# Products of constants in TensorE's waits at six norms of a two-block transformer

## What is computed

```python
for layer in range(2):                       # first block
    h = rmsnorm(x, g_mix[layer])             # norm "mix0", "mix1"
    x = x + three_attention_branches(h @ w_in[layer]) @ w_out[layer]
    h2 = rmsnorm(x, g_mlp[layer])            # norm "mlp0", "mlp1"
    x = x + square(relu(h2 @ w_up[layer])) @ w_down[layer]
x = rmsnorm(x, g_final)                      # norm "final"
x = layer_norm(ALPHA * x + gated_deltanet(x), ln_g[0, 0], ln_b[0, 0])      # "ln00"
x = layer_norm(ALPHA * x + swiglu(x), ln_g[0, 1], ln_b[0, 1])              # "ln01"
x = layer_norm(ALPHA * x + window_attention(x), ln_g[1, 0], ln_b[1, 0])    # "ln10"
x = layer_norm(ALPHA * x + moe_swiglu(x), ln_g[1, 1], ln_b[1, 1])          # "ln11"
```

## Time and profile before

| | |
|---|---|
| median of 3 runs | 2503.48 us (2501.76 to 2505.6) |
| time of the profiled execution | 2501.3 us |
| its span | 2499.6 us |
| mean granted TensorE clock | 0.985 |
| TensorE busy | 2406.9 us of the span |
| VectorE, ScalarE, GpSimd busy | 1750.8, 1420.4, 137.5 us |

### The profile page before, as it was taken

One profiled execution on the slowest core, in us unless ns is written; L12 is line 12 of the kernel. 1 busy time (PEld: TensorE's weight loads), 2 busy tenths in 40 slices (PEclk: granted clock), 3 DMA queues, 4 the chain that ended last, 5 costly groups with the idle time before them and its releaser, 6 DMA issues. The chain is left out here.

```text
span 2499.6 us, 34680 instructions
## 1 busy us (share of the span) xinstructions
PE 2406.9 (96%) x13819; PEld 2051.7 (82%) x13819; DVE 1750.8 (70%) x2029; ACT 1420.4 (57%) x1629; POOL 137.5 (6%) x177
## 2 busy tenths in 40 slices
PE   7999899999998999998999889999999999999998
PEld 6797699888777998777998778888888888888886
DVE  4456655544676555576545578898889889988988
ACT  4544544453455444433444457777777777777776
POOL 0102200000121000050000000000000000000000
PEclk9999999999999999899999899999999999999999
DMA  8343445533344555405566339999999999999997
GB/s 294 106 148 123 168 177 197 182 135 113 131 148 179 185 202 140 100 1 186 171 196 197 104 118 318 366 365 366 367 366 366 363 363 364 364 357 357 366 365 252
DMA packets 392784, 585.54 MB, mean 234 GB/s; under 512 B 21232, under 2 KB 286896, under 8 KB 392496
## 3 DMA queue, kind: packets, MB, share of 16 engines
q1 hardware_dynamic: 392624, 583.33, 68.8%
HBM read 579.09 MB, written 4.19 MB: 233 GB/s over the span
## 5 line engine op out<-in xcount | busy, mean ns | idle before, releaser
L3588 DVE TENSOR_TENSOR moe_low<-ring,moe_high 128x2048 fp32r<-128x2048 f32 x288 | 658.5, 2289 | 90.3 <-ACT moe_high L3544 86.2
L3544 ACT CAST moe_high<-ring 128x2048 fp32r<-128x2048 f32 x288 | 548.3, 1907 | 140.7 <-PE bank L3472 69.7
L3472 PE MATMUL bank<-moe_high,moe_xh 128*128 128x512 f32 x896 | 239.7, 389 | 1.0 <-PEq L3186 1.0
L3472 PE MATMUL bank<-moe_low,moe_xh 128*128 128x512 f32 x896 | 239.9, 390 | 0.0
L3472 PE MATMUL bank<-moe_high,moe_xl 128*128 128x512 f32 x896 | 239.5, 389 | 0.0
L3472 PEld LDWEIGHTS bank<-moe_high,moe_xh 128*128 128x128 f32 x896 | 168.0, 188 | 36.0 <-issue 1.1
L3472 PEld LDWEIGHTS bank<-moe_high,moe_xl 128*128 128x128 f32 x896 | 168.2, 188 | 35.0
L3472 PEld LDWEIGHTS bank<-moe_low,moe_xh 128*128 128x128 f32 x896 | 168.2, 188 | 34.9
L2132 DVE TENSOR_TENSOR chain_low<-ring,chain_high 128x2048 fp32r<-128x2048 f32 x48 | 110.0, 2291 | 117.8 <-ACT chain_high L2105 117.8
L2105 ACT CAST chain_high<-ring 128x2048 fp32r<-128x2048 f32 x44 | 84.1, 1912 | 142.1 <-PE bank L2076 108.2
L3478 PE MATMUL bank<-moe_high,moe_hh 128*128 128x512 f32 x444 | 127.4, 408 | 0.6 <-DVE moe_hl L3623 0.6
(11 more groups left out here) (545 smaller groups left out, 4918.7 us busy)
## 6 DMA issues: line engine op xcount, KB each, us to landing
ring<-in_moe_w_gate SPq DMA_DIRECT2D x199, 512.0 KB, 6.3
ring<-in_moe_w_up SPq DMA_DIRECT2D x199, 512.0 KB, 8.3
ring<-in_moe_w_down SPq DMA_DIRECT2D x95, 1024.0 KB, 8.9
ring<-in_w_in SPq DMA_DIRECT2D x21, 2048.0 KB, 8.0
ring<-in_w_down SPq DMA_DIRECT2D x14, 2048.0 KB, 7.8
ring<-in_w_up SPq DMA_DIRECT2D x10, 2048.0 KB, 8.1
xT<-in_moe_w_down SPq DMA_DIRECT2D x17, 1024.0 KB, 8.6
xT<-in_moe_w_gate SPq DMA_DIRECT2D x31, 512.0 KB, 6.6
```

What stands on the lines that cost most here:

```text
L3472: mm = pe.matmul(core.banks[i % 2][:], (xl if other_low else xh)[:, place(m), 4 * part + c, :], wt[:, c, :], start=(part == 0 and j == 0 a ...
L3544: act.copy(unit(high, u), ring.raw(u)).then_inc(s["weight_high"], 1)
L3588: dve.tensor_tensor(unit(low, u), ring.raw(u), unit(high, u), ALU.subtract)\
```

## The change

`turn_rows` looks up a triple of counts for its norm in a new table: how many idle products stand ahead of the first turn, between the turns, and behind the second. Each place gets a bank of its own: ahead, the columns that the first transpose writes; between, the columns that the second turn's first transpose writes; behind, columns of the first of the other four banks. ln10 keeps its counts. mix0 (the start) has none.

```diff
+IDLE = {"mlp0": (0, 18, 3), "mix1": (0, 21, 12), "mlp1": (0, 18, 3), "final": (0, 21, 8), "ln00": (0, 28, 0),
+        "ln01": (50, 7, 10), "ln10": (0, 13, 13)}
...
-    def turn(self, pe, src, ready=None, idle=(0, 0, 0), idle_bank=None):
+    def turn(self, pe, src, ready=None, idle=(0, 0, 0), idle_banks=(None, None, None)):
...
             if ready is not None and k == 0:
-                idle_products(self.core, pe, idle_bank, idle[t])
+                idle_products(self.core, pe, idle_banks[t], idle[t])
                 pe.wait_ge(ready[t], 1)
...
-        idle_products(self.core, pe, idle_bank, idle[NT])
+        idle_products(self.core, pe, idle_banks[NT], idle[NT])
...
     def turn_rows(self, pe):
-        idle, bank = ((0, 13, 13), self.core.banks[0][:, 0:P]) if self.row == "ln10" else ((0, 0, 0), None)
-        self.turn(pe, self.dst, (self.s["normed0"], self.s["normed1"]), idle, bank)
+        turned, other = self.banks[0], self.core.banks[4 if self.banks[0] is self.core.banks[0] else 0]
+        self.turn(pe, self.dst, (self.s["normed0"], self.s["normed1"]), IDLE.get(self.row, (0, 0, 0)),
+                  (turned[:, 0:P], turned[:, P:2 * P], other[:, 0:P]))
```

## The result

The changed kernel takes 2513.68 us (median of 8 runs, 2511.18 to 2515.81), beside 2503.43 us for the kernel before (8 runs, 2497.71 to 2506.09). The ratio is 1.0048, 95% interval 1.0036 to 1.0059: slower by 9 to 15 us. 2512.9 us was forecast, in a range of 2507 to 2518. The number was right; one step of its sum was not. In the pair of profiled executions a chance difference of 5.2 us hid that, and the timed runs show only part of what the step left out, as told at the end.

The account below looks back on a forecast made before the run. TensorE was taken as the bound. Site terms 1.84 (mlp1) + 0.81 (mlp0) + 2.52 (ln00) + 0.79 (mix1) + 0.97 (final) + 2.50 (ln01) = 9.4 us, set on the 2503.48 us median, gave 2512.9 us, range 2507 to 2518.

Parts of the forecast that it names:

- TensorE is the bound and a late turn makes the end late: Whole kernel: TensorE, busy 96% of the span, bounds the end; lateness at an earlier norm reaches it unless something absorbs it.
- rival 3: Expert stage waits for its weights and makes good a late start: same time, about 2503.5 us; 4%.
- 0.224 us for a product, two records: Price of one idle product at full clock, from ln10's 13 products: 26 records in 3.07 us.
- Rival 1: At the norms, products fit the waits and the clock comes back: 9.3 us gained, about 2494 us; 4%.
- The formula that the prediction set beside the rows: Warm product as N/2.4 + 2.5 ns: 0.056 us for 128 columns, against 0.224 us from ln10's rows.
- The delays between the turns: Products exceeding the waits make second turns late: 1.84 us at mlp1, 1.85 at mlp0, 2.93 at ln00.
- The clock comes back: At norms with half-clock stretches, filled waits restore full clock; credits such as 1.04 us at mlp0, 0.41 at ln00.
- rival 2: At the norms the clock falls all the same; delays stay, credits go: 2520 us; 9%.
- one of the prediction's own signs of being wrong: The prediction is wrong if the clock is below 1.00 at mix1 and ln01.
- ScalarE's copies are in time: At mix1, copies don't delay the first product, 3.6 us after the turn's start; at final it came after 2.10.
- Rival 4: Only half the loss arrives, as half-clock stretches elsewhere vanish or copies pace the passes: 2506 to 2508 us; 5%.
- the bounds: Above: 2520.3 us without clock credit, worst 22.7 us added; below: pacing copies hide perhaps 1 us, half-clock shifts 3 to 5.

Follow-up runs that it names:

- The doubled site: The changed kernel with 36 products instead of 18 between the turns of mlp1; a single execution, 2519.77 us.
- the counts that fit: Against the kernel before: idle products sized at 0.224 us each to fit the waits, none behind except ln10's; 2491.96 us, ratio 0.9973; again 2494.21 us, 0.9969.
- the narrow ones: The changed kernel with products of 64 columns instead of 128, all counts as they are; 2517.62 us, ratio 1.0063 to the kernel before.

## Why the prediction was right, and where it was not

**TensorE is the bound and a late turn makes the end late:** right. The doubled site added 4.01 us at its place and none of it came back; rival 3 (a later stage takes it up) is out. From the expert stage's first product to the end of the span it is 992.9 to 993.0 us in all fourteen profiles.

**0.224 us for a product, two records:** right, 0.223. Rival 1 (the products fit) is out as a description of the change, but with counts for this price it is what happens: 0.3% faster, with 4 to 5 us at the sites of the 9 that it was given. The formula that the prediction set beside the rows (the Trainium skill, "TensorE: Matmul & The Clock Gate", section "Back-to-back issue gap") is given there for an isolated product, and the section says itself that it counts too little at small widths. The prediction was right to go by the rows.

**The delays between the turns:** right. mlp1 +1.62 for 1.84; ln00 +2.25 for 2.52. What is missing I had not taken off: the 25th product comes 4.69 us after a turn that follows other work (with or without products behind it) and 4.93 us after one that follows a wait, both at full clock.

**The clock comes back:** right in the first two executions of the change, at all six sites; rival 2 is out there. In the third, mix1 is at 0.91, one of the prediction's own signs of being wrong, and 1.3 us longer. So it is right in the main, and not each time.

**"ScalarE's copies are in time":** this step failed, for mix1, and with it the sums of final and ln01, which went by it. I took the copies to follow the transposes, since the timeline gives the release of TensorE by `x_high` and nothing about what releases `x_high`. The section on the kernel says the same, that each pair of transposes releases a copy. At mlp0, mlp1 and ln00 that is all; at mix1, final and ln01 the copies stand behind the barrier as well, and it is the later. With the products ahead of it, the 25th product comes 8.56 us (mix1), 7.46 (final) and 7.89 (ln01) behind the second turn. I had 6.3, 5.4 and 5.9: 3.59, 2.69 and 3.14 to the first product, and 2.73 for the next 24. The missing term is 2.2 + 2.0 + 2.0 = 6.3 us, before rounding: 1.1 to 1.4 at each because the copies start late, and 0.9 to 1.0 because the first pass then runs at their pace. In the timelines, taking the products away or past the barrier moved it as the barrier theory says. Rival 4 and the bounds had copies that pace the passes hide part of the delay; at these three norms they added to it. The kernel before already had the evidence, in ScalarE's timeline at mix1, which I had not asked for:

```profile
498.49 2.05 ACT L408 CAST x_high<-bank 128x512 fp32r<-128x512 f32 x4 [3.61 <-PEq L740]
```

The copies' wait is ended by TensorE's sequencer at the end of the block, 2.57 us after a turn that itself lasts 1.97. At mlp1, in the middle of a block, no such meeting stands between turn and copies, and there the products behind did cost nothing.

**Why the time was right all the same.** In the profiled pair it was luck. Forecast +9.4, the sites say 14.9 between the two first profiles; there, 5.2 us came back ahead of the first norm, where the change has no part, and the spans differ by 10.5. The other two pairs of profiled executions (the first of them from different chips) differ by 10.8 and 25.9. The timed runs give 12 us (9 to 15) and 11 (7 to 16). With the missing term the forecast would have been 9.4 + 6.3 = 15.7, and the mean over three profiles is 16.4; both lie at or above the upper ends of these intervals. I didn't settle whether that is the draw of a few executions or whether something outside the sites gives a few us back: outside the sites and past the first turn the profiles agree within 1129.8 to 1132.7 us for five of six and 1136.3 for one. For the other versions the difference to the kernel before is, by sites and by time: 9.2 and 9.0 without the products behind, 5.4 and 8.2 with these alone, -5.1 and -6.7, then -4.1 and -7.8, for the counts that fit, 19 and 16 for the narrow ones. So the two differ by up to 4 us, to either side, and the gap of the change is of that size.

## What to carry to other kernels

Size filler work by what one call costs in the trace (records per call times their pitch), and compare it with the wait's idle time; an over-filled wait costs its excess in full where the engine is the bound. Ask of each wait not only how long it is but which side of a barrier its end lies on: filler behind the last real work of a block delays every engine that has work behind the barrier, one for one, and the wait stays as long as it was. When the effect is a few microseconds in 2500, compare stretches within profiles, since executions of one program differ by as much.

## What the runs showed of the hardware

At a granted clock of 1.00 the products of 128x256 have two paces. Groups of eight follow each other every 0.94 to 0.95 us in the profile before and every 0.91 in the profile after, at the same place:

```profile
107.03 1.10 PE L964 MATMUL bank<-x_high,attention_low 128*128 128x256 f32 x8
107.98 1.10 PE L964 MATMUL bank<-x_high,attention_high 128*128 128x256 f32 x8
```

```profile
107.42 1.07 PE L970 MATMUL bank<-x_high,attention_high 128*128 128x256 f32 x8
108.33 1.07 PE L970 MATMUL bank<-x_low,attention_high 128*128 128x256 f32 x8
```

Each pace holds over tens of microseconds, and which stretches have which differs between executions of one program; over 50 us it makes 2 us. Two executions of the kernel before show the same: side by side they drift apart by 2.1 us between 100 and 160 us. With the half-clock stretches that come and go (6.7 or 3.4 us at mix1; 6.7, 3.4 or none near 52 us) it makes up the 5.2 us of the early part. What sets the pace stays open.
